# Twelve sets of up-weight forms built once and fetched as bf16, attention outputs loaded through GpSimd's queue, and fetches for the down projection spread

## The reference

```python
def token_mixer(u, ...):
    proj = u @ w_in        # q,k,v of 8 stick-breaking and 8 forgetting heads, forget logits, g_sb, g_fx
    ...                    # both attentions, causal, heads of 128 -> o_sb, o_fx [S, 1024]
    merged = sigmoid(g_sb) * (o_sb @ w_branch_sb) + sigmoid(g_fx) * (o_fx @ w_branch_fox)
    return merged @ w_out

def swiglu(u, w_gate, w_up, w_down):
    return (silu(u @ w_gate) * (u @ w_up)) @ w_down

h = x + rms_norm(token_mixer(rms_norm(x, g1), ...), g2)
h = h + rms_norm(swiglu(rms_norm(h, g3), ...), g4)
```

## Time and profile before

| | us |
|---|---|
| median of 3 runs | 4331.17 |
| lowest, highest run | 3908.25, 4536.22 |
| profiled execution | 3944.87 |
| its span (core 0, slowest) | 3943.3 |
| spans of the other cores | 3859.9 to 3925.6 |

### The profile page before, as it was taken

One profiled execution on the slowest core, in us unless ns is written; L12 is line 12 of the kernel. 1 busy time (PEld: TensorE's weight loads), 2 busy tenths in 40 slices (PEclk: granted clock), 3 DMA queues, 4 the chain that ended last, 5 costly groups with the idle time before them and its releaser, 6 DMA issues.

```text
span 3943.3 us, 62875 instructions; the slowest of 8 cores (3859.9 to 3943.3 us)
## 1 busy us (share of the span) xinstructions
PE 3656.9 (93%) x21193; PEld 1849.9 (47%) x21572; DVE 1740.5 (44%) x2150; ACT 1487.7 (38%) x2339; POOL 786.4 (20%) x697
## 2 busy tenths in 40 slices
PE   5999999998799989999988888999998998999994
PEld 2566666665544434444433333444443443444442
DVE  3666777776621100222338897344456760000114
ACT  3567878876721113111333343233333430111110
POOL 0000000000011210443006732122224440001322
PEclk9889999999899999999999998899999998999997
DMA  7336665436544454776559865233346548448995
GB/s 212 62 62 97 104 101 90 82 69 76 116 84 81 76 125 136 163 172 145 178 163 270 272 199 175 86 107 107 107 128 236 198 136 214 103 101 199 211 224 174
DMA packets 328491, 556.10 MB, mean 141 GB/s; under 512 B 184688, under 2 KB 215792, under 8 KB 313072
## 3 DMA queue, kind: packets, MB, share of 16 engines
q1 hardware_dynamic: 273760, 359.06, 32.6%
q0 software_dynamic: 33680, 155.24, 21.8%
q10 hardware_dynamic: 20736, 37.76, 2.7%
HBM read 547.78 MB, written 102.76 MB: 165 GB/s over the span
## 4 chain that ended last, share of the span: by engine, by line
PE 77%; DMA 9%; DVE 6%; issue 3%; ACT 2%; SPq 1%; DVEq 0%; POOL 0%; ACTq 0%; POOLq 0%
PE ps L80 77%; DMA mh<-mixs 2%; DVE form L80 1%; DMA OT<-OTs 1%; SPq L80 1%; DMA Ost<-On 1%; DMA WT<-W 1%; DVE In L80 1%; DMA hb<-hs 1%; DMA stage<-wgu_s 1%; DVE uT L80 1%; DMA as<-ad 0%; DVE F L80 0%; ACT sq L80 0%; ACT L80 0%
## 5 line engine op out<-in xcount | busy, mean ns | idle before, releaser
L80 PE MATMUL ps<-F,form 128*128 128x512 bf16 x4829 | 1116.4, 392 | 85.5 <-DVE ao L80 24.4
L80 PEld LDWEIGHTS ps<-F,form 128*128 128x128 bf16 x4928 | 491.5, 100 | 705.5 <-issue 214.2
L80 PE MATMUL ps<-as,wd 128*128 128x512 bf16 x2765 | 622.8, 382 | 19.2 <-DMA as<-ad 16.0
L80 PE MATMUL ps<-uT,wbf 128*128 128x512 bf16 x1992 | 493.4, 391 | 26.4 <-DVE uT L80 16.1
L80 DVE TENSOR_TENSOR form<-stage 128x1024 bf16<-128x1024 f32 x292 | 420.7, 1457 | 167.9 <-PE ps L80 148.1
L80 PE MATMUL ps<-uT,wgA 128*128 128x512 bf16 x2012 | 449.6, 379 | 1.8
L80 PEld LDWEIGHTS ps<-as,wd 128*128 128x128 bf16 x2816 | 275.9, 98 | 355.8 <-issue 27.7
L80 POOL TENSOR_TENSOR sn<-sn,sn 128x512 f32<-128x512 f32 x176 | 257.1, 1465 | 692.2 <-ACT sn L80 679.4
L80 DVE TENSOR_TENSOR m<-ps,s 128x512 f32<-128x512 f32 x128 | 88.4, 691 | 550.9 <-PE ps L80 548.3
L80 PEld LDWEIGHTS ps<-uT,wbf 128*128 128x128 bf16 x2048 | 200.8, 100 | 249.3 <-issue 74.2
L80 PEld LDWEIGHTS ps<-uT,wgA 128*128 128x128 bf16 x2048 | 200.1, 98 | 241.4
(11 more groups left out here) (107 smaller groups left out, 3351.3 us busy)
## 6 DMA issues: line engine op xcount, KB each, us to landing
stage<-wgu_s SPq DMA_DIRECT2D x68, 2048.0 KB, 9.7
wd<-wfd_t POOLq DMA_DIRECT2D x32, 1408.0 KB, 13.1
wgA<-wg_t POOLq DMA_DIRECT2D x64, 512.0 KB, 6.1
wbf<-wqkv_t POOLq DMA_DIRECT2D x48, 512.0 KB, 6.8
ad<-ao SPq DMA_DIRECT2D x176, 128.0 KB, 4.5
as<-ad SPq DMA_DIRECT2D x22, 1024.0 KB, 20.0
xs<-xq SPq DMA_DIRECT2D x16, 1024.0 KB, 12.7
wgA<-wb_t POOLq DMA_DIRECT2D x32, 512.0 KB, 6.6
```

The source lines that it names most:

```text
L80: ins = getattr(eng, meth)(**kw)
```

## The change

Five edits.

(a) OT1's first load is issued by POOL, in four DMAs of three heads each at `t0` 12, 16, 20 and 28; `load_OT` is issued by POOL as well. (b) The first gate tile of the first gates phase (4 groups of 8 matmuls, chunk 0, c = 0) is emitted during the last pair's units from 24 on. (c) `P5(0)` gets 24 side items. Each loads half of an up-weight stage (1 MB), makes its seven forms 512 wide (five on DVE, two on ACT) in the single tile `pf`, and stores them in a DRAM tensor `fd` (896 KB). Segments 0 and 2 then fetch the up forms of i = 0 to 11 from `fd`, 256 KB each on SP, into eight slots `dring`; gate sets still go through a stage, with one slot instead of two, and form 6 moves from POOL to DVE. Pre-made forms of the first set may be emitted earlier. (d) `wo` blocks 0 to 2 are loaded ahead of the reload of OT and of the stage, and block c + 3 is issued behind block c's matmuls. (e) The loads for the down projection are issued at steps 40 and 64 (`wd`) and 88, 104, 120 and 136 (`as`) of segment 2. Renamed tiles share DMA semaphores (`sat`).

```diff
@@ attention, last pair
-                kb.dma(SP, OT1.ds, OT1.t[:, 0:6, :], ...)
-                kb.dma(SP, OT1.ds, OT1.t[:, 6:12, :], ...)
+            if i == NH - 1 and t0 in (12, 16, 20, 28):
+                a_ = {12: 0, 16: 3, 20: 8, 28: 11}[t0]
+                p_ = a_ if a_ < 8 else a_ - 2
+                kb.dma(POOL, OT1.ds, OT1.t[:, p_:p_ + 3, :], OTs[a_:a_ + 3, :, 0:1024].rearrange("h p t -> p h t"),
+                       reads=[OT_res[hh][c] for hh in range(a_, a_ + 3) for c in range(2)], writes=[OT1.r])
...
+                fl2 = Filler(gate_tile(wg[0][0], 0, 0) + gate_tile(wg[0][1], 0, 1), 2 * 15)
@@ load_OT
-            kb.dma(SP, tile.ds, tile.t[:, a_:a_ + len(hs_), :],
+            kb.dma(POOL, tile.ds, tile.t[:, a_:a_ + len(hs_), :],
@@ P5
             if first:
-                gates(0)
                 gates(1)
@@ WOUT
-            if c + 2 < KC:
-                load_wo(c + 2)
...
+            if c + 3 < KC:
+                load_wo(c + 3)
@@ before P5(0)
+    ps = [at(WO + 20 * i, f"ps{i}", [128, 4, 512], F32, dma=True) for i in range(2)]
+    pf = at(WO + 28, "pf", [128, 7, 512], BF16, dma=True)
+    def pre_load(j):
+        if j < 2 * N0:
+            i, hv = j // 2, j % 2
+            kb.dma(SP, ps[j % 2].ds, ps[j % 2].t[:, :, :],
+                   wgu_s[i, 1].rearrange("p (a b) -> p a b", a=4)[:, :, hv * 512:(hv + 1) * 512], writes=[ps[j % 2].r])
+    def pre_make(j):
+        def f():
...
+            pre_load(j + 1)
+            src = ps[j % 2]
+            for x, p in enumerate(PORD):
+                a_, b_, op = FORM_A[p]
+                o = pf.t[:, x, :]
...
+                    kb.op(ACT, "activation", dict(out=o, in_=src.t[:, a_, :], func=AF.Copy), reads=[src.r],
+                          writes=[pf.r])
...
+                    kb.op(DVE, "tensor_tensor", dict(out=o, in0=src.t[:, a_, :], in1=src.t[:, b_, :], op=op),
+                          reads=[src.r], writes=[pf.r])
+            kb.dma(SP, pf.ds, fd[i, :, :, hv * 512:(hv + 1) * 512].rearrange("x p b -> p x b"), pf.t[:, :, :],
+                   reads=[pf.r], writes=[fd_res[i][hv]])
...
     load_OT(0, OT2)
-    P5(0, nofill)
+    fl = Filler([pre_make(j) for j in range(2 * N0)], 29)
+    P5(0, fl)
+    fl.flush()
...
     load_wo(0)
     load_wo(1)
+    load_wo(2)
     load_OT(1, OT1)
@@ produce
+        while npr[1] < len(prodD):
+            s_, p = prodD[npr[1]]
+            if not freeD or use_at[(s_, p)] > now + 16 or (s_ > nS[0] and now < dring_from[0]):
+                break
...
+            kb.dma(SP, dst.ds, dst.t[:, :, :].rearrange("p a b -> p (a b)"), fd[sets[s_][1], PORD.index(p)],
+                   reads=fd_res[sets[s_][1]], writes=[dst.r])
...
-            if not due and (not free or now < ready[s_] or k_ >= most or use_at[(s_, p)] > now + 14):
+            if not due and (not freeS or now < ready[s_] or k_ >= most or use_at[(s_, p)] > now + 15):
...
-                E = POOL if p == 6 and not both else DVE
-                kb.op(E, "tensor_tensor", dict(out=o, in0=sl.t[:, a_, :], in1=sl.t[:, b_, :], op=op),
+                kb.op(DVE, "tensor_tensor", dict(out=o, in0=sl.t[:, a_, :], in1=sl.t[:, b_, :], op=op),
@@ segment 2
-    load_wd(0, 0)
-    load_wd(1, 1)
-    for gi in range(4):
-        load_a(0, gi)
     for n in range(seg_end[1], seg_end[2]):
         gu_step(n)
+        j = n - seg_end[1]
+        if j in (40, 64):
+            load_wd(j // 64, j // 64)
+        if j in (88, 104, 120, 136):
+            load_a(0, (j - 88) // 16)
```

More of the change, by code:

```diff
@@ L740, in at, with gate_tile, half @@
         return Slot(kb, name, shape, dtype, dma=dma)
+    def gate_tile(w, tc, bi):
+        bt, br_ = banks[bi]
+        def half(hf_):
+            def f():
+                kb.group(PE, [("matmul", dict(out=bt[:, :], lhsT=w.t[:, k, :], rhs=uT.t[:, k, tc * 512:(tc + 1) * 512],
+                                              start=(k == 0), stop=(k == KC - 1)))
+                              for k in range(8 * hf_, 8 * hf_ + 8)], reads=[w.r, uR[tc]], writes=[br_])
+            return f
+        return [half(0), half(1)]
     def load_A(c):
@@ L1107, in _emit, with mk_dring @@
     MAT = FC // 2
-    N0 = 12
-    stage = [at(76 + 16 * i, f"stage{i}", [128, 4, 1024], F32, dma=True) for i in range(2)]
+    stage = [at(76, "stage0", [128, 4, 1024], F32, dma=True), None]
     formw = [at(56 + 2 * i, f"form{i}", [128, 8, 128], BF16) for i in range(10)]
-    FORM_A = {1: (0, 3, ALU.add), 5: (0, 1, ALU.add), 2: (2, 3, ALU.add), 3: (0, None, None), 4: (3, None, None),
-              6: (2, 0, ALU.subtract), 7: (1, 3, ALU.subtract)}
+    dring_ds = [kb.dsem(f"formd{i}") for i in range(8)]
+    def mk_dring():
+        out = [at(92 + 2 * i, f"formd{i}", [128, 8, 128], BF16) for i in range(8)]
+        for sl, ds in zip(out, dring_ds):
+            sl.ds = ds
+        return out
+    dring = mk_dring()
     ORDER = (5, 2, 1, 3, 4, 6, 7)
@@ L1130, in _emit @@
         seg_end.append(len(steps))
-    PORD = (5, 2, 6, 1, 3, 4, 7)
-    prods = [(s_, p) for s_ in range(len(sets)) for p in PORD]
+    nS = [len(segs[0]), len(segs[0]) + len(segs[1])]
+    is_d = [m == 1 and i < N0 for m, i, _ in sets]
+    slot_of = [(s_ - nS[0]) % 2 if nS[0] <= s_ < nS[1] else 0 for s_ in range(len(sets))]
+    staged = [s_ for s_ in range(len(sets)) if not is_d[s_]]
+    prodS = [(s_, p) for s_ in staged for p in PORD]
+    prodD = [(s_, p) for s_ in range(len(sets)) if is_d[s_] for p in PORD]
@@ L1133, in _emit @@
     use_at = {sp: n for n, sp in enumerate(steps)}
-    ready = [0, 0] + [10 ** 9] * len(sets)
-    free = list(range(10))
+    ready = [10 ** 9] * len(sets)
+    nxt = {s_: next((x for x in staged if x > s_ and slot_of[x] == slot_of[s_]), None) for s_ in staged}
+    freeS, freeD = list(range(10)), list(range(8))
     held = {}
-    npr = [0]
-    def load_stage(s_):
-        if s_ < len(sets):
-            m, i, _ = sets[s_]
-            sl = stage[s_ % 2]
-            kb.dma(SP, sl.ds, sl.t[:, :, :].rearrange("p a b -> p (a b)"), wgu_s[i, m], writes=[sl.r])
@@ L1145, in produce, with load_stage @@
-    def produce(now, most):
+    npr = [0, 0]
+    def load_stage(s_, now):
+        m, i, hs_ = sets[s_]
+        sl = stage[slot_of[s_]]
+        kb.dma(SP, sl.ds, sl.t[:, :, :].rearrange("p a b -> p (a b)"), wgu_s[i, m], writes=[sl.r])
+        ready[s_] = now + (4 if len(hs_) == 2 else 7)
+    def produce(now, most):
+        while npr[1] < len(prodD):
+            s_, p = prodD[npr[1]]
+            if not freeD or use_at[(s_, p)] > now + 16 or (s_ > nS[0] and now < dring_from[0]):
+                break
+            npr[1] += 1
+            j = freeD.pop(0)
+            dst = dring[j]
+            held[(s_, p)] = (dst, j)
+            kb.dma(SP, dst.ds, dst.t[:, :, :].rearrange("p a b -> p (a b)"), fd[sets[s_][1], PORD.index(p)],
+                   reads=fd_res[sets[s_][1]], writes=[dst.r])
@@ L1160, in produce @@
             else:
-                E = POOL if p == 6 and not both else DVE
-                k_ += 1 if E is DVE else 0
-                kb.op(E, "tensor_tensor", dict(out=o, in0=sl.t[:, a_, :], in1=sl.t[:, b_, :], op=op),
+                k_ += 1
+                kb.op(DVE, "tensor_tensor", dict(out=o, in0=sl.t[:, a_, :], in1=sl.t[:, b_, :], op=op),
                       reads=[sl.r], writes=[dst.r])
-            if p == PORD[-1] and s_ + 2 < len(sets):
-                load_stage(s_ + 2)
-                ready[s_ + 2] = now + (4 if both else 7)
-    load_stage(0)
-    load_stage(1)
+            if p == PORD[-1]:
+                if s_ == nS[1] - 1:
+                    drop(stage[1])
+                    dring[:] = mk_dring()
+                    dring_from[0] = now
+                if nxt[s_] is not None:
+                    load_stage(nxt[s_], now)
+    dring_from = [10 ** 9]
+    load_stage(0, -8)
+    ready[0] = -8
     pre_items = [(lambda n: (lambda: produce(n, 1)))(n - 8) for n in range(7)]
@@ L1245, in gu_step @@
             evict_gu(s_, p, h)
-        free.append(held.pop((s_, p)))
+        (freeD if is_d[s_] else freeS).append(j)
+        if n == seg_end[0] - 1:
+            drop(*dring)
+            stage[1] = at(92, "stage1", [128, 4, 1024], F32, dma=True)
+            load_stage(nS[0] + 1, n)
         produce(n, 2 if len(hs_) == 2 else 1)
@@ L1293, in _emit @@
         al.kill(r_)
-    drop(*stage, *formw, *sg, *snap[0], *snap[1], *aout)
+    drop(stage[0], *dring, *formw, *sg, *snap[0], *snap[1], *aout)
     for i in range(4, NSL):
```

58 lines of the change are left out of this document (38 added, 20 removed).

## The result

The changed kernel takes 3858.36 us (median of 4 runs, 3855.46 to 4296.87). The kernel before, run beside it, had 4536.22, 3908.25, 4331.17 and 3918.91. Both kernels have executions of over 4,000 us in which the cores of a die show a lower granted clock, whatever the kernel; the ratio is taken over the others. It is 0.9856, with a 95% interval of 0.982 to 0.9893: 1.4% faster. Forecast were 3842 us and, against the profiled execution of before, 2.6%. So the time lies in the range of 3765 to 3940, the gain is about half of that forecast, and "faster by over 2%", which had the largest chance, did not happen.

The account below looks back on a forecast made before the run. The prediction took the kernel to be bound by TensorE, so only PE's gaps and slow stretches could go. Its terms, -10 - 8 + 12 - 60 - 15 - 5 - 17 = -103, took 3944.87 to 3842 us, range 3765 to 3940.

Parts of the forecast that it names:

- (a): Attention: issuing OT1's loads from POOL frees SP for the transposes PE waits for; -10 us, bounds 0 and -12.
- (b): Attention's tail: first gate tile moved there, OT2 loaded earlier from POOL; -8 us, bounds 0 and -10.
- (d): Output projections: `wo` blocks loaded earlier remove PE's waits in WOUT(0) and WOUT(1); -15 and -5 us.
- (e): Start of segment 2: spreading down's loads removes PE's wait behind SP's `as` loads; -17 us, bounds -10 and -17.
- faster by over 2%: Whole kernel: the outcome of a time below 3866 us, given a chance of 0.66.
- (c1): First gates phase: 24 items making and storing forms, at a 13.0 us cycle against 12.5; +12 us.
- (c2): Segment 0: no start waits for forms, faster mh loads, less DVE work; -18, -10 and -32, sum -60 us.
- first rival: First gates phase is paced by `pf`'s store, a 17 us cycle making it 108 us longer; 3938 us, 14%.
- second rival: Segment 0 stays paced by its transfers, so only the start and 12 us return; 3872 us, 14%.
- (c3): Segment 2: fetched forms gain nothing, since PE idles only 1.4 us there; 0 us.
- rival of denser work drawing a lower clock: Gate, up and down work: denser PE work lowers the granted clock throughout, +364 us; 4206 us, 6%.

Follow-up runs that it names:

- x1: The kernel before with the OT, gate tile, wo and down-load edits only, no stored forms; 3864.3 us, ratio 0.9894.
- x11: The changed kernel run once more, unchanged; lowest of six executions 3893.03 us, median 4276.84 us.
- x5: The changed kernel with the loads of segment 0's residual pass issued four items ahead instead of two; 3858.6 us.
- x10: The changed kernel with `load_OT` issued by SP again, the gate tile staying in the attention's tail; 3885.31 us.
- x8: The changed kernel with the first gate tile moved back from the attention to the first gates phase; 3874.53 us.
- x9: The changed kernel without stored forms, but with the first set's forms made ahead of segment 0; 3852.31 us.
- x3: The changed kernel with two `pf` tiles in turn and their forms tracked one by one; 3832.53 us, ratio 0.9806.
- x12: Second run of the changed kernel with two `pf` tiles tracked in parts and residual loads four items ahead; 3844.25 us, ratio 0.9783.
- x7: The kernel before with only OT1's first load moved to POOL, in four parts; 3930.1 and 4072.81 us.

## Why the prediction was right or wrong

| term | forecast | measured | from |
|---|---|---|---|
| (a) | -10 | -6 | PE's waits for WT |
| (b) | -8 | -3 | P5(0), before 332.4, x1 329.2 |
| (c1) | +12 | +33 | P5(0), x1 329.2, after 362.3 |
| (c2) | -60 | -46 | segment 0, 387.0 to 340.9 |
| (d) | -15, -5 | -17, -4.5 | WOUT(0), WOUT(1) |
| (e) | -17 | -17.5 | segment 2 |
| sum | -103 | -61, and -79 by the spans | |

The -79 is the difference of the median spans, 3907.3 to 3828.6; the 18 between it and -61 are the attention's other 7.5 us, which lie within its spread, 2.5 in segment 1 and the down projection, and that medians of stages do not add up exactly.

**(c1), the step that failed.** The mechanism was on record as the danger and as the first rival: item j + 1 may not write before item j's store has landed, and "a DVE wait for `pf` proves the first rival". That wait is there, 143.5 us of 300. So the rival's mechanism decided, at a price between the forecast's +12 and its +108. The term that failed is the cycle of the single tile: 13.0 us were taken, and 14.0 were measured (median of the cores, 13.8 to 14.2; 14.1 to 14.5 on cores 4 to 7 of x11). 24 x 1.5 = 36, near the +33. I took "the middle" between 14.6, by shares with the neighbours' 46.7%, and 11.3, which knew nothing of the casts beside; there was no ground for a middle. Nor was 14.6 right: it would have given 24 x 2.1 = +50, and that core 3 shows 14.65 over three stores is chance. Its parts were off in opposite directions. Forms and copies take 5.3 us, not 4.4: DVE's 0.69 us each is less than the 886 ns taken, but ACT's two copies and the hand-overs stand in the same chain, and they had been left out. The store's landing is 9.4 to 9.8 us on core 3 (10.2 by the shares), and 12.5 - 5.3 = 7.2 were to be had. That PE is delayed through ACT (copies ahead of the sigmoids) is as predicted.

**(c2), right in kind, a quarter too large.** Its absolute end, 338 us, was nearly met (340.9). The start gave 13.6 instead of 18, the rest 30.0 instead of 42. I had counted segment 0 of before as 398 us on one core; by the same cut core 0 has 392.3 and the median of the cores 387.0. Five us of that was core 0's own. The other six are records that its trace lacks: the forecast counted recorded matmuls up to 2430, and the weight loads, which are complete, show the 1344th issued at 2432.1 with only 1316 matmuls on record (before, core 0, 2040 to 2432.2):

```profile
L80 PEld LDWEIGHTS ps<-F,form x1344: 94/98/153, 2040.3 to 2432.1; 128*128 128x128 bf16 x192
L80 PE MATMUL ps<-F,form x1316: 376/379/635, 2040.4 to 2432.1; 128*128 128x512 bf16 x188
```

So segment 0 ended at 2432, not at 2438. mh's landing went from 12.6 to 11.9 (forecast 12.0). The second rival, that transfers pace the residual pass, has the mechanism in its favour (x5: the wait moves to the stage at once) but not the size: 46 us came back, not 30. No run splits the 30.0 us between the faster loads and DVE's shorter work, so that the forecast's division was right is not shown.

**(b), read from a core that was not typical.** The forecast removed 7.7 us between OT2's old and new arrival, from the earlier trace rows's wait of 3.07 us on core 0. The other cores of before wait 0.2 to 1.1 us, as core 5 here (PE's timeline of before):

```profile
1079.59 1.46 PE L80 MATMUL ps<-OT,wgA 128*128 128x512 bf16 x6
1081.27 5.77 PE L80 MATMUL ps<-OT,wgA 128*128 128x512 bf16 x26 [0.22 <-DMA OT<-OTs]
```

There OT2 was hidden, and all that could be gained was the moved tile's 6.9 us less the wait that it lays bare. In the changed kernel that wait is 3.1 to 6.1 us: POOL cannot issue the second load before the first has landed and the last output's transpose is through (POOL's timeline, core 3, and PE's):

```profile
1098.55 0.72 POOL L80 DMA_DIRECT2D OT<-OTs  x1 [49.13 <-DVE On L80]
1104.12 0.70 POOL L80 DMA_DIRECT2D OT<-OTs  x1 [4.86 <-DMA Ost<-On]
...
1109.31 7.06 PE L80 MATMUL ps<-OT,wgA 128*128 128x512 bf16 x26 [3.13 <-DMA OT<-OTs]
```

6.9 - 3.1 = 3.8 agrees with the 3.2 of the table. That the tile alone brings nothing was right: up to the 16th matmul on OT it takes 17.8 us before, 18.2 with the tile alone (x10), 16.9 with the queue alone (x8) and 15.0 with both (medians).

**(a) and (d), right in kind for another reason.** The forecast read the 16.13 and 25.53 us of the earlier trace rows as issuing. They are waits: the first OT1 load was issued at 1020.7, the second when the first had landed, and each issue took 0.38 us or less (before, core 0, SP's waits of 1020 to 1045, and the loads' durations in ns):

```profile
SPq L75 <- DMA OT<-OTs: 15.3, 1, 15.3
...
L80 SPq DMA_DIRECT2D OT<-OTs x2: 365/374/382, 1020.7 to 1036.4; - x2
```

What stood behind them in SP's stream was late all the same, so moving them away helped, as forecast, and the sentence of (a) that "the issuing time is the 16.13 us itself" is wrong. In (a) three or four shorter waits, mostly of 1 to 5 us, took half the place of the long one.

**(d), (e), (c3).** (d), (e) and the nothing of (c3) came within 2.5 us each. WOUT(1)'s 4.5 us appear only with (c): in x1 and x9, which have (d) but two stages to load, WOUT(1) is 127.8 and 129.2.

**The clock** did not get worse: the cores' mean granted clock is 0.970 to 0.980, and no core has the stretch of 0.81 of the earlier trace rows. The rival of denser work drawing a lower clock fell, also in x3 and x12, which are denser still. The stretch came back only in x7, on the same two cores 0 and 1 (segment 1 in 506.8 and 512.2 us, 484.6 on others), and x7 has none of the denser stages.

**The base.** 2.6% was forecast against a profiled execution of 3944.87 us, and the ratio is taken over runs of 3908 and 3919. Its cores were slow on the whole: their median span is 3907.3 us, that of another execution of the same kernel, beside x12, 3884. So some 23 of the 79 us by spans are that execution's and not the edits'. 1.4% of 3913.6 is 56 us, near the 61 of the terms. Of the 47 us between the forecast 103 and these 56 the terms account for 42: (c1) 21, (c2) 14, (b) 5, (a) 4, less 2 of (d) and (e). That the time came so near is in part luck: the base was 31 us too high and the gain 47 too large. The sentence that put all on the profiled execution's scale served for the time, where these two errors partly cancel (3842 against 3858), and was wrong for the chances, which go by the ratio: the forecast's own limit of 2% was drawn at 3866 where it should have been near 3835, 0.98 of 3913.6.

**What stays open.** Why cores of one execution differ by 40 us in the attention, and what segment 0's last 44 us over its 297 of matmuls would need: longer look-ahead moved the wait to the stage, and a second stage slot was not tried, since the ring for fetched forms holds its place.

## What to carry to other kernels

Work moved into a phase that PE bounds is not free because its engines are idle there: compute its cycle, from first write of the buffer to the landing of the store, on DMA engines as loaded as they will be, and give it a second buffer wherever that comes near the time between two items. When two estimates of a wait differ, the middle has no ground; start from the one that counts the traffic beside it, and price the range. A long row of DMA issues on an in-order stream can be waits for landings: ask what each issue waited for before calling it issuing time. And read a wait on several cores before pricing it, count weight loads where matmul records may be missing, and put a gain on the scale of the executions it will be compared with.
